# Transposing through VectorE and DRAM instead of TensorE in the mixing stage of a transformer block

## The reference

```python
h = rms_norm(x, attn_norm_w)
proj = h @ w_in                      # (256, 5184)
hq, hf, hi, hg, c_q, c_kv, k_r = split(proj)       # 4 x 1024, 512, 512, 64
o_a = hgrn2_mixer(hq, hf, hi, hg, lower_bounds, hgrn_norm_w)   # 8 heads of 128
# latent attention, 8 heads: q = rms_norm(c_q) @ w_uq, (k, v) = rms_norm(c_kv) @ w_ukv,
# query and key of 128 + 64 (rotated) elements, normalised per head, chunked causal mask
o_b = mla_mixer(c_q, c_kv, k_r, cos, sin, ...)
x = x + concat([o_a, o_b]) @ w_out
h = rms_norm(x, ffn_norm_w)
gate, up = split(h @ w_gate_up)
x = x + (silu(gate) * up) @ w_down
```

## Time and profile before

| | |
|---|---|
| median of 3 runs | 1125.22 us (1125.12 to 1125.36) |
| the profiled execution | 1124.67 us, of which 1122.9 us span |
| TensorE busy | 1113.2 us, 99% |
| VectorE busy | 886.8 us, 79% |
| ScalarE busy | 640.5 us, 57% |
| DMA, mean over the span | 204 GB/s |

### The profile page before, as it was taken

The page is one execution under the profiler, slowest core; times in us unless marked ns, Lnnn a source line. Parts: engine busy times, 40 slices in busy tenths (PEclk is TensorE's granted clock), DMA queues, the critical chain, the costliest instruction groups (busy, mean ns, idle before and its releaser), DMA issues.

```text
span 1122.9 us, 15465 instructions
## 1 busy us (share of the span) xinstructions
PE 1113.2 (99%) x5265; PEld 937.8 (84%) x5265; DVE 886.8 (79%) x1198; ACT 640.5 (57%) x907; POOL 51.1 (5%) x134
## 2 busy tenths in 40 slices
PE   7999999999999999999999999999999999999998
PEld 7988888888888888888888888888888888888887
DVE  5578786587876667688888888888988879889777
ACT  7566776668664556454554554554554555555553
POOL 3000000000000000000000000000000010000000
PEclk9999999999999999999999999999999999999999
DMA  8666455545555455667777677777777686666655
GB/s 267 192 196 189 158 159 156 164 141 170 197 177 168 153 187 169 212 212 234 225 229 237 222 232 238 222 229 236 224 235 226 224 276 217 207 206 199 211 190 169
DMA packets 107239, 228.99 MB, mean 204 GB/s; under 512 B 8201, under 2 KB 19250, under 8 KB 106930
## 3 DMA queue, kind: packets, MB, share of 16 engines
q1 hardware_dynamic: 101346, 209.30, 58.9%
q0 software_dynamic: 5536, 18.88, 5.8%
q10 hardware_dynamic: 304, 0.14, 0.0%
HBM read 218.32 MB, written 9.96 MB: 203 GB/s over the span
## 4 chain that ended last, share of the span: by engine, by line
PE 97%; DVE 2%; DMA 1%; ACT 0%; issue 0%; SPq 0%; DVEq 0%; ACTq 0%
PE side L1919 25%; PE main L1693 22%; PE side L1921 12%; PE main L1696 11%; PE side L1891 4%; PE side L1892 4%; PE side L1893 4%; PE main L1893 3%; PE main L1891 3%; PE main L1892 3%; PE side L1817 1%; PE side L1716 1%; DMA raw<-in_w_in 1%; PE side L1764 0%; PE side L1765 0%; DVE w_lo L1084 0%
## 5 line engine op out<-in xcount | busy, mean ns | idle before, releaser
L977 ACT CAST w_hi<-raw 128x1024 fp32r<-128x1024 f32 (+1 forms) x245 | 241.6, 990 | 172.2 <-PE side L1919 104.9
L1532 DVE TENSOR_TENSOR w_lo<-raw,w_hi 128x1024 fp32r<-128x1024 f32 (+1 forms) x245 | 275.4, 1139 | 21.9 <-ACT w_hi L977 21.6
L1084 DVE TENSOR_TENSOR w_lo<-raw,w_hi 128x1024 fp32r<-128x1024 f32 (+3 forms) x156 | 178.5, 1154 | 107.9 <-ACT w_hi L757 105.6
L757 ACT CAST w_hi<-raw 128x1024 fp32r<-128x1024 f32 (+3 forms) x156 | 153.7, 993 | 142.5 <-PE main L1693 137.6
L1693 PE MATMUL main<-w_hi,hT_hi 128*128 128x512 f32 (+2 forms) x448 | 173.4, 388 | 1.7 <-DVE hT_lo L1105 1.4
L1696 PE MATMUL main<-w_hi,hT_lo 128*128 128x512 f32 (+2 forms) x448 | 169.1, 378 | 0.0
L1921 PE MATMUL side<-w_hi,hT_lo 128*128 128x512 f32 x400 | 155.6, 389 | 0.0
L1919 PE MATMUL side<-w_hi,hT_hi 128*128 128x512 f32 x400 | 155.6, 389 | 0.0
L1693 PE MATMUL main<-w_lo,hT_hi 128*128 128x512 f32 (+2 forms) x448 | 114.6, 377 | 0.0
L1919 PE MATMUL side<-w_lo,hT_hi 128*128 128x512 f32 x400 | 106.9, 389 | 0.0
L1693 PEld LDWEIGHTS main<-w_hi,hT_hi 128*128 128x128 f32 x448 | 84.7, 189 | 15.5 <-DVE hT_lo L1105 1.8
(11 more groups left out here) (279 smaller groups left out, 1819.0 us busy)
## 6 DMA issues: line engine op xcount, KB each, us to landing
raw<-in_w_gate_up SPq DMA_DIRECT2D x176, 512.0 KB, 4.8
raw<-in_w_down SPq DMA_DIRECT2D x88, 512.0 KB, 4.5
raw<-in_w_in SPq DMA_DIRECT2D x64, 512.0 KB, 3.8
raw<-in_w_out SPq DMA_DIRECT2D x32, 512.0 KB, 3.7
raw<-in_w_in SPq DMA_DIRECT2D x15, 384.0 KB, 4.5
squares<-hiddenT POOLq DMA_DIRECT2D x11, 512.0 KB, 5.0
hiddenT<-squares POOLq DMA_DIRECT2D x44, 128.0 KB, 5.3
raw<-in_w_ukv SPq DMA_DIRECT2D x8, 512.0 KB, 3.9
```

What stands on the lines that cost most here:

```text
L757: copy(w_hi[:, slot, 0:n], raw[:, slot, 0:n]).then_inc(s_hi, 1)
L977: copy(w_hi[:, n % RING, 0:cols], src).then_inc(s_hi, 1)
L1084: tt(w_lo[:, slot, 0:n], raw[:, slot, 0:n], w_hi[:, slot, 0:n].bitcast(F32), ALU.subtract)\
L1532: tt(w_lo[:, n % RING, 0:cols], src, w_hi[:, n % RING, 0:cols].bitcast(F32), ALU.subtract)\
```

## The change

The latents, the recurrence queries of both groups, the output of the first group, and the queries and keys of the first two pairs (`MOVED_HEADS = 2`) are transposed in the way of the feed-forward part. A new step `swap` has VectorE transpose blocks of 32 x 32 into a buffer (for the latents `hbT` and `hkT`, for the recurrence queries half of `E`, for the output `hgate`, for queries and keys a new tile `heads`), after which POOL writes it to DRAM and reads it back in four parts. The steps `lat_t`, `turn(g, 0, t)`, `o_t(0, j)`, `q_t(j)` and `k_t(j)` for j < 2 no longer have a share of TensorE; ScalarE (and VectorE, for the lo parts) reads the landed buffer. These steps, and the scores of the first two pairs, get later positions:

| step | position before | after |
|---|---|---|
| swap lat 0, 1 | - | 19, 27 |
| lat_t(0, 0), (0, 1) | 22, 22 | 26, 27 |
| lat_t(1, 0), (1, 1) | 30, 30 | 34, 35 |
| swap hq 0; swap q 0; swap k 0 | - | 34; 36; 46 |
| q_t(0), k_t(0) | 39, 49 | 41, 51 |
| scores(0), scores(1) | 50, 53 | 52, 55 |
| swap q 1; swap k 1 | - | 56; 66 |
| q_t(1), k_t(1) | 59, 69 | 61, 71 |
| scores(2), scores(3) | 70, 73 | 72, 75 |
| swap o 0; swap hq 1 | - | 81; 84 |
| turn(1, 0, t), turn(1, 1, t) | 89, 91 | 90, 91 |

`softmax`, `probs_t` and `attend` of heads 0 to 3 move by two as well. turn(0, 0, t) stays at 45 and o_t(0, j) at 95. Within a position the order is that of the list; `swap` stands behind the step that makes its data.

The core of the diff: the schedule; POOL's `swap` and the order of its calls; ScalarE's wait and its copies of `q_t` and `k_t`; VectorE's transposing and its halved lo parts (shown for `lat_t`, for `o_t(0, j)` alike); TensorE's wait ahead of the scores:

```diff
     for i in range(2):
         e = END[("lat", i + 1)]
-        s += [(e + 1, ("lat_a", i)), (e + 2, ("lat_b", i))] + [(e + 5, ("lat_t", i, n)) for n in range(2)]
+        s += [(e + 1, ("lat_a", i)), (e + 2, ("lat_b", i)), (e + 2, ("swap", "lat", i))]
+        s += [(e + 9 + n, ("lat_t", i, n)) for n in range(2)]
...
-        s += [(q - early, ("q_a", j)), (q - 1 if early else q + 1, ("q_b", j)), (q + 4, ("q_t", j))]
+        moved = 2 * (j < MOVED_HEADS)
+        s += [(q - early, ("q_a", j)), (q - 1 if early else q + 1, ("q_b", j))]
+        s += [(q + 1, ("swap", "q", j))] * (moved > 0) + [(q + 4 + moved, ("q_t", j))]
...
-            p = k + 5 + (j > 1) + (7 if j == 2 else 3) * (h % 2)
+            p = k + 5 + moved + (j > 1) + (7 if j == 2 else 3) * (h % 2)
...
-        s += [(e + 2 + 2 * g + n * (1 + g), ("turn", g, n, t)) for n in range(2) for t in range(NT)]
+        s += [(e - g if g else END[("hq", g)] + 1, ("swap", "hq", g))]
+        s += [(e + 2 + 3 * g + n, ("turn", g, n, t)) for n in range(2) for t in range(NT)]
...
-        s += [(p, ("o_a", g)), (p + 1, ("o_b", g))]
+        s += [(p, ("o_a", g)), (p + 1, ("o_b", g))] + [(p + 1, ("swap", "o", g))] * (g == 0)
...
+            def swap(*key):
+
+                n, at = SWAP[key], swap_of[key]
+                wide = at.shape[2]
+                pool.wait_ge(s_swap, n + 1)
+                pool.dma_start(swapped[n, :, :, :, 0:wide].rearrange("a c b x -> (a c) b x"), at).then_inc(s_parked, 16)
+                pool.wait_ge(s_parked, 16 * (n + 1))
+                for b in range(P // Q):
+                    pool.dma_start(at[Q * b:Q * (b + 1), :, :], swapped[n, :, :, b, 0:wide].rearrange("a c x -> c a x"))\
+                        .then_inc(s_landed, 16)
...
+            swap("lat", 0)
+            swap("lat", 1)
+            swap("hq", 0)
+            for j in range(MOVED_HEADS):
+                swap("q", j)
+                swap("k", j)
             pool.wait_ge(s_lbused, 1)
             pool.wait_ge(s_side, USE[("join8", 0)] + 1)
             pool.dma_start(lb[:, :, :], hgrn_lb[:, GW:2 * GW].partition_broadcast(P)).then_inc(s_lbin, 16)
 
+            swap("o", 0)
+            swap("hq", 1)
...
+            def landed(*key):
+                act.wait_ge(s_landed, MOVED * (SWAP[key] + 1))
...
+                    if j < MOVED_HEADS:
+                        key = (kind[0], j)
+                        landed(*key)
+                        straight = swap_of[key][:, :, 0:2 * NT * Q].rearrange("p a (t h r) -> p t h a r", t=NT, r=Q)
+                        turned = swap_of[key][:, :, 2 * NT * Q:].rearrange("p a (t r) -> p t a r", r=Q)
+                        for h in range(2):
+                            copy(by_quarter(plain[:, 2 * j + h, :]), straight[:, :, h, :, :])
+                        if kind == "k_t":
+                            copy(by_quarter(kTr[:, j, :]), turned).then_inc(s_heads, 1)
+                            return
...
+            def swap(key, src):
+
+                nc.vector.transpose(swap_of[key].rearrange("p b (n r) -> p n b r", r=Q),
+                                    src.rearrange("p t (k b c) -> p (t k) b c", b=P // Q, c=Q)).then_inc(s_swap, 1)
...
+                    split_lo(s, [(by_quarter(mT_lo[:, k + n, :])[:, t, :, :], swapped_tile(("lat", i), 2 * j + n)[:, t, :, :],
+                                  by_quarter(mT_hi[:, k + n, :])[:, t, :, :], col + n) for n in range(2) for t in range(NT)])
...
                 elif kind == "scores":
                     h = a[0]
-                    given(("k_t", h // 2, 1))
+                    if h // 2 < MOVED_HEADS:
+                        pe.wait_ge(s_heads, 2 * (h // 2) + 2)
+                    else:
+                        given(("k_t", h // 2, 1))
```

## The result

The changed kernel takes 1141.78 us (median of 4 runs, 1139.64 to 1142.09) against 1125.26 (1125.12 to 1125.36): a ratio of 1.0142, 95% interval 1.0126 to 1.0158, or 16.5 us more. The forecast was 1134.9 with a range of 1126.5 to 1141.0. The sign was right, the size was not, and the range missed by 0.8. The profiled execution spans 1140.1 us, 17.2 more than the one of before.

What follows compares the result with a forecast made beforehand. TensorE was taken to bound the kernel. Level 1 late by 9.3, less 3.1 of later transposes, plus 1.2 and 2.3 for later waits, gave +9.7 us on 1125.2: 1134.9, range 1126.5 to 1141.

Steps and rivals of the forecast that it cites:

- The bound and the 7.0 us: TensorE, busy for 99% of the span, bounds the kernel; taking out 64 transposes of 0.11 us each gives 7.0 us.
- Work on queues with room: Work added on VectorE, ScalarE and POOL; POOL's trips put at nothing, sharing DMA with weight loads at 0, at most 1.
- Trips of 13.7 and 13.0, ends 12 and 15: Time from start of transposing to landing: 13.7 us for full trips, 13.0 for heads, with 12 and 15 as ends.
- none was under 14: Said of the eleven feed-forward trips, against the 0.09 case that all trips are covered and the kernel gets faster.
- The estimate of 8.5 us: Heads' trip by the skill's 2.0 us plus bytes over 436 GB/s; the change would be nearly free; rejected on the trace.
- Step 1: First latents: landing at 67.5, ScalarE stands 2.8 us, q_b(0) ends at 104.0; TensorE's stalls, about 6 us, not summed.
- Step 2: Queries of pair 0: landing at 117.0, ScalarE blocks 7 us at position 41, hf_a(0) starts at 120.4, 8.1 late.
- Step 3: Recurrence chain without slack: level 1 starts at about 149.0 instead of 139.65, 9.3 us late; TensorE stands about 4.5 us.
- rival 3: The wait ahead of scores(0) also lowers TensorE's clock, costing 1 to 3 us more: 1137; chance 0.15.
- Step 4: Behind level 1: -3.1 for transposes still gained, +1.2 at scores(2), +2.3 for two transposings on VectorE near granule 88.

Runs made afterwards that it cites:

- slack_c: Kernel before with only the first latents (copies at 28, 30), the queries of pair 1 and the output of group 0 moved: 1122.65 us, ratio 0.9977.
- ghost_heads: Kernel before plus VectorE's transposings and DRAM trips for queries and keys of pairs 0 and 1, nobody waiting for them: 1124.93 us, ratio 0.9999.
- q0_later: Changed kernel with ScalarE's copies of the queries of pair 0 at position 48 instead of 41: 1138.02 us, ratio 1.0115.
- hq_o_only: Kernel before with only the recurrence queries of both groups and the output of group 0 moved: 1127.28 us, ratio 1.0021.
- slack_b: Kernel before with both latents (the first's copies at 28), the queries of pair 1 and the output of group 0 moved: 1127.10 us, ratio 1.0017.
- heads_only: Kernel before with only the queries and keys of pairs 0 and 1 moved, with their later positions: 1132.03 us, ratio 1.0061.
- warm: Changed kernel with 36 identity products on TensorE ahead of the wait of scores(0): 1144.64 us, ratio 1.0168.
- order_only: Kernel before with only the later positions of pairs 0 and 1, all transposes still on TensorE: 1128.53 us, ratio 1.0030.
- lat_later: Changed kernel with the copies of the first latents at positions 28 and 30 instead of 26 and 27: 1137.24 us, ratio 1.0105.
- after_order: Changed kernel with copies of pair 0's queries at 48, scores(0) at 53 behind level 1, scores(3) and softmax(3) at 73 and 74: 1137.83 us, ratio 1.0109.
- all_later: Changed kernel with the first latents' copies at 28 and 30, pair 0's queries at 48, scores(3) and softmax(3) at 73 and 74: 1133.83 us, ratio 1.0075.
- warm_short: Changed kernel with 16 identity products on TensorE ahead of the wait of scores(0): 1138.88 us, ratio 1.0124.

## Why the size was wrong, step by step

- **The bound and the 7.0 us.** Right: 0.11 for a transpose agrees with slack_c (2.5 us for 22).
- **Work on queues with room, at nothing.** Right for POOL, the traffic and VectorE's work on the heads (ghost_heads 1.00). Wrong for the weight loads between 102 and 118 us, which were put at 0 to 1: ScalarE waits 2.91 and 3.67 for them in the changed kernel, covered there by the landing, and 2.18 in q0_later, not covered. Wrong too for the 1.25 us transposings at VectorE's tight places (hq_o_only, slack_b).
- **Trips of 13.7 and 13.0, ends 12 and 15.** The latents took 14.8 (transposing from 54.17, landed 68.92), the queries of pair 0 12.1 (105.75 to 117.85), the keys of pair 1 13.5 (207.19 to 220.69). Trips of the heads ranged from 10.9 (heads_only) to 14.1 (warm). The feed-forward rows were the right choice, though ScalarE waited for the landing in one of those eleven trips only, so "none was under 14" isn't shown by them. The estimate of 8.5 us by the Trainium skill (DMA: Bandwidth & Descriptors, Anatomy of one DMA) fits none of these trips.
- **Step 1.** Landing 67.5, measured 68.9; q_b(0) 104.0, measured 105.7. Stalls of granules 31, 33, 34 and 40 were named rightly, 38 was 35. That they are no term of the sum holds as long as the pause follows.
- **Step 2.** 117.0 and 120.4, measured 117.85 and 121.33. ScalarE was to stand 7 us for the landing; it stood 3.67, and before that 6.6 us for two weight tiles.
- **Step 3.** scores(0) at 147.8, measured 148.70; TensorE to stand some 4.5 us in a row, measured 3.98 with 0.23. The lateness was 0.9 short. **Then the first failed term: the products behind the pause were taken at their old durations** (1.12, 2.05). They took 2.72 and 3.45, 3.1 us with the granule behind. That is rival 3, at 0.15, with a price of 2 us. The Trainium skill (TensorE: Matmul & The Clock Gate, The HAM clock gate) says that idle time halves the clock. The trace agrees: 1.00 ahead of the pause and a mean of 0.54 in the 5 us behind it. As the forecast itself expected a pause of 4.5 us, the fall of the clock should have been part of it.
- **Step 4.** Given as +0.4 (-3.1 + 1.2 + 2.3), measured 16.9 - 13.2 at granule 52 = +3.7. scores(2) cost 1.9 for 1.2, granule 88 1.9 for 2.3. **The second failed term is the one that is missing**, the cost of the new order: softmax(3) behind q_b(2), 1.91 + 0.23, and 0.79 for `stage_r`, 2.9 us. order_only shows both without a trip.

Sum: 9.7 + 0.9 + 3.1 + 2.9 + 0.7 - 0.4 = 16.9, the shift from granule 123 on. The range missed, by less than 1 us, because its upper end took in a longer trip, but neither of these terms.

**Left open:** how much of the 6.0 us of a load near 112 is contention with the trips and how much the other loads, since no kernel here kept VectorE's lateness and took the traffic away.

## What to carry to other kernels

Work taken from the bounding engine is gained only where that engine isn't about to wait for a chain of other engines of fixed length; measure that chain between two points and count what the bound has left to do beside it. When a step is moved by some positions, list its new neighbours on every engine: here the order alone cost 3.6 us, where the whole change costs 16.5. And when a forecast contains a pause of TensorE of some microseconds, price what follows it at half clock.

## What was not expected of the hardware

A pause of 3.7 to 4.0 us lowered the granted clock in all six kernels that had one. Of shorter pauses the length doesn't tell: one of 2.1 us at granule 40 lowered it in three profiled executions and not in four, with much the same program up to there. In lat_later one of 2.70 us left it at 1.00, and one of 1.92 us lowered it to 0.70, which six other kernels with the same pause (1.91 or 1.92) don't show. Its two marks, a product behind the second, and the stretch from 240 us:

```profile
121.52 0.47 PE L1836 MATMUL main<-w_hi,hT_hi 128*128 128x512 f32 x1 [2.70 <-ACT hlf L983]
...
239.07 0.55 PE L1920 MATMUL side<-ident,probs 128*128 128x128 f32 x3 [1.92 <-DVE probs L1423]
...
239.73 0.63 PE L1839 MATMUL main<-w_hi,hT_lo 128*128 128x512 f32 x1
```

```profile
240.00:245.00 5.00, 5.00 (x20) 4.00 (x20) 4.17 (x15) 4.45 (x9) 0.00 (x0) 0.70 0.31 99
```

At granule 40, from 106 to 112 us, the changed kernel has 1.00; so have, behind the same pause, lat_later, after_order and all_later. q0_later has 0.78, warm 0.72 and warm_short 0.76. The stretch in q0_later, and its products of 512 columns, whose spacing doubles from 0.23 to 0.43 about 1.3 us behind the pause:

```profile
106.00:112.00 6.00, 4.09 (x13) 3.29 (x14) 5.93 (x7) 1.05 (x1) 1.81 (x3) 0.78 0.91 231
```

```profile
108.90 0.39 PE L1836 MATMUL main<-w_hi,hT_hi 128*128 128x512 f32 x1
109.13 0.44 PE L1839 MATMUL main<-w_hi,hT_lo 128*128 128x512 f32 x1
109.36 0.63 PE L1836 MATMUL main<-w_hi,hT_hi 128*128 128x512 f32 x1
109.79 0.63 PE L1839 MATMUL main<-w_hi,hT_lo 128*128 128x512 f32 x1
```

It is at full speed again by granule 42, and lost 1.6 us (granules 40 to 42 take 9.9 us against 8.3). Such a short pause is a cost that comes in some executions only. The trip of the queries of pair 0 varies as well: it took 12.1 us in the changed kernel's profiled execution, 12.8 in that of warm_short and 14.1 in that of warm, with the same steps up to there. Either can be why the changed kernel's runs spread by 2.4 us; this was not tested.
